# A fifth seven-product unit per chunk, and the residual additions moved from VectorE to ScalarE copies and adding transfers

## The reference, cut to what matters

```python
h2 = _rmsnorm(x, ffn_norm[l])
ff = jax.nn.silu(jnp.einsum('bsd,df->bsf', h2, w_gate[l])) * jnp.einsum('bsd,df->bsf', h2, w_up[l])
x = x + jnp.einsum('bsf,fd->bsd', ff, w_down[l])
```

## Time and profile before

| | us |
|---|---|
| median of 3 runs (2177.16 to 2179.44) | 2178.67 |
| the profiled execution | 2179.32 |
| its span, first to last instruction | 2177.5 |
| TensorE busy | 2160.8 |
| VectorE busy | 1715.2 |
| ScalarE busy | 1083.4 |
| GpSimd busy | 22.2 |

### The profile page before, as it was taken

The page is one execution under the profiler, slowest core; times in us unless marked ns, Lnnn a source line. Parts: engine busy times, 40 slices in busy tenths (PEclk is TensorE's granted clock), DMA queues, the critical chain, the costliest instruction groups (busy, mean ns, idle before and its releaser), DMA issues.

```text
span 2177.5 us, 27179 instructions
## 1 busy us (share of the span) xinstructions
PE 2160.8 (99%) x10826; PEld 1845.2 (85%) x10826; DVE 1715.2 (79%) x1938; ACT 1083.4 (50%) x1144; POOL 22.2 (1%) x24
## 2 busy tenths in 40 slices
PE   9999999999999999999999999999999999999998
PEld 7899988888888888888888999888888888888886
DVE  5576774788898888889755867747888898888887
ACT  5454543554554544555453545435545554545544
POOL 0000000000000000000000000000000000000000
PEclk9999999999999999999999999999999999999999
DMA  7544455555665566566555434555665655565564
GB/s 251 179 135 130 141 177 184 181 197 194 200 200 196 193 202 202 193 202 201 191 176 174 139 115 154 176 188 181 199 200 194 204 199 193 194 206 197 195 206 159
DMA packets 221679, 402.77 MB, mean 185 GB/s; under 512 B 13440, under 2 KB 53664, under 8 KB 221472
## 3 DMA queue, kind: packets, MB, share of 16 engines
q1 hardware_dynamic: 220880, 400.90, 56.0%
q10 hardware_dynamic: 720, 0.78, 0.1%
HBM read 399.54 MB, written 2.10 MB: 184 GB/s over the span
## 4 chain that ended last, share of the span: by engine, by line
PE 95%; DMA 2%; DVE 1%; issue 1%; ACT 1%; SPq 0%; ACTq 0%; DVEq 0%; POOLq 0%; POOL 0%
PE bank L1015 19%; PE bank L1017 19%; PE bank L1016 19%; PE bank L694 10%; PE bank L696 10%; PE bank L695 10%; PE bank L654 2%; DMA stage<-in_w_in 1%; PE bank L819 1%; PE bank L760 0%; PE bank L883 0%; PE bank L871 0%; PE bank L761 0%; PE bank L762 0%; PE bank L770 0%
## 5 line engine op out<-in xcount | busy, mean ns | idle before, releaser
L1536 DVE TENSOR_TENSOR w_lo<-stage,w_hi 128x2048 fp32r<-128x2048 f32 (+4 forms) x319 | 679.6, 2132 | 269.0 <-ACT w_hi L1179 268.5
L1179 ACT ACTIVATE w_hi<-stage 128x2048 fp32r<-128x2048 f32 (+4 forms) x319 | 569.4, 1787 | 388.6 <-DMA stage<-in_w_down 192.2
L694 PE MATMUL bank<-w_hi,xt_hi 128*128 128x512 f32 (+4 forms) x1048 | 376.8, 359 | 6.1 <-DVE xt_lo L1597 4.3
L696 PE MATMUL bank<-w_hi,xt_lo 128*128 128x512 f32 (+4 forms) x1048 | 369.4, 352 | 0.0
L695 PE MATMUL bank<-w_lo,xt_hi 128*128 128x512 f32 (+4 forms) x1048 | 369.1, 352 | 0.0
L1015 PE MATMUL bank<-w_hi,xt_hi 128*128 128x512 f32 x812 | 316.5, 390 | 0.1
L1017 PE MATMUL bank<-w_hi,xt_lo 128*128 128x512 f32 x812 | 316.0, 389 | 0.0
L1016 PE MATMUL bank<-w_lo,xt_hi 128*128 128x512 f32 x812 | 315.9, 389 | 0.0
L1015 PE MATMUL bank<-w_hi,f_hi 128*128 128x512 f32 x696 | 271.3, 390 | 0.2 <-DVE f_lo L1945 0.2
L1017 PE MATMUL bank<-w_hi,f_lo 128*128 128x512 f32 x696 | 270.9, 389 | 0.0
L1016 PE MATMUL bank<-w_lo,f_hi 128*128 128x512 f32 x696 | 270.8, 389 | 0.0
(11 more groups left out here) (258 smaller groups left out, 2820.5 us busy)
## 6 DMA issues: line engine op xcount, KB each, us to landing
stage<-in_w_gate SPq DMA_DIRECT2D x176, 512.0 KB, 3.8
stage<-in_w_up SPq DMA_DIRECT2D x176, 512.0 KB, 4.7
stage<-in_w_down SPq DMA_DIRECT2D x174, 512.0 KB, 4.6
stage<-in_w_in SPq DMA_DIRECT2D x96, 384.0 KB, 3.7
stage<-in_w_out SPq DMA_DIRECT2D x64, 512.0 KB, 4.6
stage<-in_w_in SPq DMA_DIRECT2D x54, 512.0 KB, 4.5
stage<-in_w_in SPq DMA_DIRECT2D x16, 320.0 KB, 3.4
stage<-in_w_q_b SPq DMA_DIRECT2D x12, 384.0 KB, 3.7
```

The lines of the kernel that those rows point to most:

```text
L694: pe.matmul(acc, a, wh[:, i, :], start=first and i == 0, stop=False)
L696: mm = pe.matmul(acc, b, wh[:, i, :], start=False, stop=last and i == len(kts) - 1)
L1179: act.activation(w_hi[s][:, 0:kts * cols], stage[s][:, 0:kts * cols], ACT.Copy).then_inc(hi_made[s], 1)
L1536: vec.tensor_tensor(w_lo[s][:, 0:kts * cols], stage[s][:, 0:kts * cols], w_hi[s][:, 0:kts * cols].bitcast(F32), ALU.subtract).then_inc(lo_ ...
```

## The change

A fifth unit of each steady chunk becomes a set: SETS = (0, 2, 3, 5, 6), PAIRS = (1, 4, 7), K_SET = 5, so that sets cover row blocks 0 to 9. Chunk 1 keeps its three sets; only the row blocks it pairs are others. In all chunks but the last, the additions to resid leave VectorE. ScalarE copies the two banks of a down unit to part_sum (four buffers of 128 x 512, two used by even units and two by odd), and GpSimd issues for each a DMA from part_sum to resid that adds (256 KB, 160 in the kernel). ScalarE waits for a buffer's earlier transfer before it copies into it again; TensorE waits for the copies (part_out) where it waited for the additions; VectorE waits for all transfers before the last chunk's additions, which stay on it. On ScalarE the copies of unit c - 1 stand ahead of preparing unit n0 + c + 3. In iteration c = 3 the copies of units 2 and 3 and `ff_turn` all stand ahead of preparing i2, where the rounding of i2 stood before `ff_turn`. On VectorE i2 is now a set, with its sums ahead of f_lo and its subtractions behind. Some buffers move in the arena.

```diff
-X_ADDS = ADDS * (1 + FF_CHUNKS)
+X_ADDS = 2 * ADDS
+COPIES = ADDS * (FF_CHUNKS - 1)
...
-SETS = (0, 3, 4, 6)
-PAIRS = (1, 2, 5, 7)
+SETS = (0, 2, 3, 5, 6)
+PAIRS = (1, 4, 7)
...
-SECOND_TILES = (8, 9), (10, 11), (12, 13), (3, 7), (14, 15)
+SECOND_TILES = (10, 11), (12, 13), (8, 9), (3, 4), (14, 15)
...
+        part_sum = [arena(f"part_sum{i}", [P, NCH], F32, 8 * SEQ + NCH * i) for i in range(4)]
...
                 def added(f, n):
 
-                    pe.wait_ge(x_added, layer * X_ADDS + 2 * ADDS + f * ADDS + n)
+                    pe.wait_ge(part_out, layer * COPIES + f * ADDS + n)
...
+                def copy_out(c, n0, chunk, turn=0):
+
+
+                    n = n0 + c
+                    act.wait_ge(used[n % 4], layer * QUADS + n // 4 + 2 + turn)
+                    for t in range(NT):
+                        i = c % 2 * 2 + t
+                        before = 16 * (2 * layer * (FF_CHUNKS - 1)) + chunk * 32 + c // 2 * 16
+                        if not (layer == 0 and n0 == U_SECOND + 8 and c < 2):
+                            act.wait_ge(part_added[i], before)
+                        act.activation(part_sum[i][:, :], bank[DOWN_BANKS[c][t]][:, :], ACT.Copy).then_inc(part_out, 1)
+
                 def down(f, n0, turn=0, sets=0, after_set=True):
+
                     for c in range(4):
                         if c == 0 and after_set:
                             silus(f + 1)
-                        prepare(n0 + c + LEAD, turn, sets,
-                                (lambda: ff_turn(f + 1, TURN_BANKS, 0)) if c == 3 else None)
+                        if c:
+                            copy_out(c - 1, n0, f, turn)
+                        if c == 3:
+                            copy_out(3, n0, f, turn)
+                            ff_turn(f + 1, TURN_BANKS, 0)
+                        prepare(n0 + c + LEAD, turn, sets)
...
+                def add_part(f, c):
+
+                    for t in range(NT):
+                        i = c % 2 * 2 + t
+                        pool.wait_ge(part_out, layer * COPIES + f * ADDS + NT * c + t + 1)
+                        pool.dma_start(resid[:, t, c * NCH:(c + 1) * NCH], part_sum[i][:, :], accum_op=ALU.add)\
+                            .then_inc(part_added[i], 16)
+
+                for f in range(FF_CHUNKS - 1):
+                    for c in range(4):
+                        add_part(f, c)
...
-                def add_down(c, n0, turn=0):
-                    n = n0 + c
-                    vec.wait_ge(used[n % 4], layer * QUADS + n // 4 + 2 + turn)
-                    for t in range(NT):
-                        part = resid[:, t, c * NCH:(c + 1) * NCH]
-                        vec.tensor_tensor(part, bank[DOWN_BANKS[c][t]][:, :], part, ALU.add).then_inc(x_added, 1)
-
                 def down(f, n0, turn=0, sets=0, after_set=True):
-
-                    def between():
-                        add_down(3, n0, turn)
-                        ff_turn(f + 1, TURN_BANKS, 0)
 
                     for c in range(4):
                         if c == 0 and after_set:
                             activate(f + 1, n0 - 8, turn)
-                        if c:
-                            add_down(c - 1, n0, turn)
-                        prepare(n0 + c + LEAD, turn, sets, between if c == 3 else None)
+                        prepare(n0 + c + LEAD, turn, sets,
+                                (lambda: ff_turn(f + 1, TURN_BANKS, 0)) if c == 3 else None)
...
-                add_down(3, U_PEEL + 8)
-                vec.wait_ge(x_added, layer * X_ADDS + X_ADDS)
+                for i in range(4):
+                    vec.wait_ge(part_added[i], 32 * (layer + 1) * (FF_CHUNKS - 1))
```

More of the change, by code:

```diff
@@ L335, in program @@
         xn = arena("xn", [P, NT, D_MODEL], F32, 16 * SEQ)
-        f_hi = [arena(f"f_hi{i}", [P, 4, SEQ], F32R, 4 * SEQ * (2 * i)) for i in range(2)]
-        f_lo = [arena(f"f_lo{i}", [P, 4, SEQ], F32R, 4 * SEQ * (2 * i + 1)) for i in range(2)]
+        f_hi = [arena(f"f_hi{i}", [P, 4, SEQ], F32R, 46 * SEQ * i) for i in range(2)]
+        f_lo = [arena(f"f_lo{i}", [P, 4, SEQ], F32R, 4 * SEQ + 46 * SEQ * i) for i in range(2)]
+        part_sum = [arena(f"part_sum{i}", [P, NCH], F32, 8 * SEQ + NCH * i) for i in range(4)]
         xs_hi = arena("xs_hi", [P, 4, K_SET, P], F32R, 16 * SEQ)
[L340 to L346, removed]
+        xs_lo = arena("xs_lo", [P, 4, K_SET, P], F32R, 26 * SEQ)
+        xs = arena("xs", [P, 4, K_SET, P], F32, 26 * SEQ)
+        kept = [arena(f"kept{i}", [P, NCH], F32, 36 * SEQ + NCH * i) for i in range(5)]
+        sums = [arena(f"sums{i}", [P, 3, NCH], F32, 46 * SEQ + 3 * NCH * i) for i in range(3)]
+        sums_lo = [arena(f"sums_lo{i}", [P, 3, NCH], F32R, 46 * SEQ + 3 * NCH * i) for i in range(3)]
+        sums_hi = [arena(f"sums_hi{i}", [P, 3, NCH], F32R, 64 * SEQ + 3 * NCH * i) for i in range(3)]
+        x_whole = arena("x_whole", [P, 2 * K_SET, SEQ], F32, 64 * SEQ)
         stage_x = arena("stage_x", [P, 4 * NCH], F32, 60 * SEQ)
@@ L417, in program @@
         down_made = sem("down_made")
+        part_out = sem("part_out")
+        part_added = [sem(f"part_added{i}") for i in range(4)]
         ms_made, rstd_made = sem("ms_made"), sem("rstd_made")
@@ L589, in load_sets @@
                         for w, at in ((w_gate, 0), (w_up, 2)):
-                            if in_set(n) or n0 == U_SECOND and i == 5:
-                                m = 3 if not in_set(n) else sets_of(n).index(i)
+                            if in_set(n):
+                                m = sets_of(n).index(i)
                                 src = w[layer, m * P:(m + 2 * K_SET) * P, bass.ds(f * NCH, NCH)]\
@@ L1135, in last_down @@
                         if not last and t == 1 and c >= 2:
-                            added(f, 4)
+                            need(x_added, X_ADDS, 2 * ADDS + 4)
                             norm_turn("norm1", range(2 * c - 4, 2 * c - 2), layer + 1)
@@ L1466, in _ @@
                         silus(FF_CHUNKS - 1)
+                    else:
+                        copy_out(c - 1, U_PEEL + 8, FF_CHUNKS - 2)
                     if c == 1 and layer == DEPTH - 1:
@@ L1472, in _ @@
                         ff_turn(FF_CHUNKS - 1, TURN_BANKS, 1)
+                copy_out(3, U_PEEL + 8, FF_CHUNKS - 2)
                 if layer < DEPTH - 1:
@@ L2128, in _ @@
                         activate(FF_CHUNKS - 1, U_PEEL, 0)
-                    else:
-                        add_down(c - 1, U_PEEL + 8)
                     if c == 1 and layer == DEPTH - 1:
```

## The result

The changed kernel takes 2224.85 us (median of 4 runs, 2223.16 to 2225.39) against 2179.02 us before (4 runs): ratio 1.021, interval 1.0198 to 1.0223. It is 45.8 us slower, where 2190 was forecast and the range ended at 2216. The 54 matmuls are gone (10,772 for 10,826), worth 12.2 us by the prediction's price, so some 58 us of delay are to be explained. TensorE's busy time shows 44 of them as idle: 60.7 us of the span for 16.7 before.

A forecast was written before the change was run, and what follows sets the result against it. TensorE was taken to bound the kernel, VectorE close behind in one stretch. From 2179.32 us: -12.2 for matmuls, -1.0 for last-chunk waits, 18 x (0.7 + 0.65) for stalls, net +11.1, so 2190; range 2167 to 2216.

The forecast's parts named there:

- The 54 matmuls: One more set per steady chunk, nine chunks a layer, two layers: 12.2 us off TensorE at 0.2267 us each.
- The sign: The whole kernel was forecast to get slower, 2190 us against 2179.32; chance of slower 0.63.
- VectorE's unchanged sum: Per chunk VectorE loses eight residual additions, 4.8 us, and the new set costs it 4.8 us.
- The schedule behind T: From T, where TensorE finishes a chunk's last down unit: i6 ready at T+31.3, wanted at T+30.85.
- i2 as a set eats the whole product: With gate/up unit i2 a set, TensorE stands still 0.7 us per chunk, all that the removed product had given.
- rival B: Additions do not delay i2's load at all: 2178.7 us, no change (2174 to 2182); chance 0.24.
- the term d: Delay of i2's load landing by adding transfers, per chunk: taken as 0.7 us, between 0 and 3.1.
- E: Rival, chance 0.12: engines serve two queues in turn, each addition beside i2's load delays it 0.78 us; 2207 to 2234 us.
- C: Rival, chance 0.09: additions land late, so copies of down unit 3 wait for buffers; 2200 to 2240 us.
- D: Rival, chance 0.13: VectorE's chain reaches i6 in time and the whole 13.2 us stay; 2166 us.
- 0 for the mixed tokens: Mixed tokens made of ten tiles for eight, once a layer: cost 0, about 2 us a layer without cover.
- The 1.0 us that I took off: In the two last chunks TensorE's waits for f_lo behind additions, 0.35 and 0.65 us, were to go.

## Why the prediction was wrong

**What held.** The sign. The 54 matmuls and VectorE's unchanged sum. The schedule behind T, from the rows of before: the run with small transfers meets it to 0.1 us at i6 (T+31.26 for T+31.3), and the run with the sets alone meets the same schedule with the additions put back. So the finding that i2 as a set eats the whole product held: almost without the transfers' data the change comes out at 2180.2, no change, near rival B's 2178.7.

**What failed: the term d**, "I take d = 0.7, about one addition's data". It measured 2.3 in the chunk shown and 1.7 to 2.3 in its neighbours. The prediction's own formula, a stall of 0.7 + d, makes 2.4 to 3.0 us of that; the loop chunks measured 2.6 to 3.1 over 62.8. So the path was right and the term on it mis-sized. Two things were wrong in it. The price of one addition: I used the chunk's rate and had 0.78 us of all engines; an adding transfer takes 1.56, and only a plain one 0.69. But the plain ones delay i2's load as much, so the price alone does not explain d. And its reach: I let it touch i2's load alone, while the load of i3 takes 9 to 10 us and, with the sets at i0, i1, i3, i5 and i6, that of i4 8.6 us. In the change itself this reach cost little (0.20 us in the chunk shown); it is what the runs that reordered the work met. The bound of 3.1 us for d did hold; the value within it was taken from the wrong end. The chunk's idle 0.41 of DMA time that I named for B is no reserve there, since the additions come while loads move.

**The rivals.** E, with d between 1.6 and 3.1 and 2207 to 2234 us, had 0.12; its numbers are what was measured. Its mechanism is not shown. It lets an addition delay the load by the addition's own DMA time, and the delay stayed the same where that time fell from 1.56 to 0.69 us. With 1.56 us in place of E's 0.78, two to four additions make 3.1 to 6.2 us, which was not measured, so the hit is in part luck. E named the rule of the Trainium skill that each engine goes round its busy queues a packet at a time (page "DMA: Bandwidth & Descriptors", section "Queues, rings and completion order"). The trace doesn't settle it: GpSimd's queue moved 218 packets and SyncE's 6 in the two microseconds from 696.00, which is no even turn, and 139 and 130 in the next two. Whether SyncE's queue had its packets ready in the first two is not shown. C happened too (61.3 us of ScalarE's waits) and was mostly covered by the late load: 4 us at the median. D needed i6 in time: with no data of transfers it was still late by 0.7 us.

**A smaller term, 0 for the mixed tokens.** It measured 2.2 us per layer, the 2 us that I had named for the case that the cover is gone. VectorE's work there ends in act_sb, for which the first pair of chunk 1 waits; I had looked at the totals, not at what is due at the end.

**The account.** 16 loop chunks by 2.06 us are 33.0; the peeled chunks, 59.99 and 61.75 us for 58.05, add 5.6; act_sb 4.4; the last f_lo waits (1.34 and 1.04 us for the earlier trace rows's 0.35 and 0.65) 1.4. That is 44.4 of 45.8. The stretches at the lower clock, two for one, are 1.7 us more and fit what is left. The 1.0 us that I took off for the last was not a gain but a loss.

**What stays open** is how the engines share between the queues, why a plain transfer delays the load as much as one that adds, and why the adding ones take more than twice the DMA time; a pacing of the additions over the whole chunk wasn't tried.

## What to carry to other kernels

A transfer that replaces an instruction isn't free because its engines idle on average: look at the DMA share of the very stretch, and count the transfer against every load issued within about ten microseconds of it. Before you move work off a busy engine, look for its own idle time. Here the kernel with seven late additions per chunk on VectorE, which is then 96% busy, gained 5 us, and the one with 160 transfers lost 46; the first also has the sets and f_lo in better places. And where a unit grows dearer, its place matters more than the sum: a set prepared while VectorE idled (i1) cost 13 us less than the same set one place on, and 4 us less once the transfers' data were gone.

## What the runs showed of the hardware

A transfer from GpSimd's queue that adds 256 KB in SBUF took 1.56 us of all 16 DMA engines and 6.4 us from issue to landing; a plain one of the same size 0.69 and 5.3 us; an adding one of 8 KB 0.26 us (1.9% of 2176 us over 160) and 3.5 us. GpSimd spent 0.88 us on issuing each adding one (1.77 us for two). A load of 1 MB beside these transfers, with the engines at a share of 1.1, landed after 8.6 to 10 us instead of 5.1, and SyncE's issue of its second half took up to 1.2 us instead of 0.47. The share given by the profile can pass 1.0: it is 1.04 in two microseconds of a load that runs alone.
